# The end of the odd mixer: who splits the up weights, who takes the last roots, and the order of the last half blocks

## What is computed

```python
for layer in range(DEPTH):
    g = norm_gains[layer]
    h = rmsnorm(x, g[0])
    mix = even_mixer(...) if layer % 2 == 0 else odd_mixer(h, w_qkv, sinks, w_out, cos, sin)
    x = x + rmsnorm(mix, g[1])
    h = rmsnorm(x, g[2])
    x = x + rmsnorm(conv_ffn(h, ffn_w_in[layer], ...), g[3])

def rmsnorm(x, g):
    return x * lax.rsqrt(jnp.mean(x * x, axis=-1) + EPS) * g
```

## Time and profile before

| | us |
|---|---|
| timed runs, median of 3 | 2566.87 |
| timed runs, lowest and highest | 2565.96 and 2571.13 |
| the profiled execution | 2568.79 |
| its span in the trace | 2567.0 |

### The profile page before, as it was taken

How to read it: one execution, slowest core, us unless ns; L and a number is a source line. 1 busy time by engine, 2 the same in 40 slices (tenths; PEclk the granted TensorE clock), 3 DMA queues, 4 the chain that set the end, 5 groups by cost and what they waited for, 6 DMA issues and landing times. The chain is left out here.

```text
span 2567.0 us, 31771 instructions
## 1 busy us (share of the span) xinstructions
PE 2373.3 (92%) x11619; PEld 1983.1 (77%) x11619; DVE 1671.2 (65%) x2408; ACT 1189.6 (46%) x1881; POOL 912.7 (36%) x670
## 2 busy tenths in 40 slices
PE   6889878989899899999999979899879999999998
PEld 5668667889777688888787867688767888887886
DVE  4564667865544788888636744556577888884365
ACT  4444777766533343443425532455423443443354
POOL 2101103401011688888200001132258888870000
PEclk9999988999999899999999989979989999999999
DMA  4001101000041122222664731221112222237475
GB/s 147 26 25 42 33 1 42 26 1 2 30 168 59 57 91 82 80 85 82 211 211 167 247 107 41 52 64 50 67 54 81 79 90 83 76 102 252 154 254 180
DMA packets 183156, 237.47 MB, mean 93 GB/s; under 512 B 14132, under 2 KB 135316, under 8 KB 183004
## 3 DMA queue, kind: packets, MB, share of 16 engines
q1 hardware_dynamic: 177440, 217.94, 26.2%
q10 hardware_dynamic: 5564, 17.52, 1.7%
HBM read 195.48 MB, written 39.94 MB: 92 GB/s over the span
## 5 line engine op out<-in xcount | busy, mean ns | idle before, releaser
L126 PE MATMUL l_ps<-l_t_hi,l_s_hi 128*128 128x512 f32 x480 | 186.7, 389 | 0.0
L126 PE MATMUL l_ps<-l_t_lo,l_s_hi 128*128 128x512 f32 x480 | 186.7, 389 | 0.0
L126 PE MATMUL l_ps<-l_t_hi,l_s_lo 128*128 128x512 f32 x480 | 186.7, 389 | 0.0
L2230 POOL TENSOR_TENSOR l_s_lo<-l_raw,l_s_hi 128x512 fp32r<-128x512 f32 x100 | 157.2, 1580 | 45.8 <-ACT l_s_hi L2134 45.8
L2230 POOL TENSOR_TENSOR l_s_lo<-l_w_sum,l_s_hi 128x512 fp32r<-128x512 f32 x80 | 168.6, 2128 | 6.1 <-ACT l_s_hi L2134 3.7
L2506 DVE TENSOR_TENSOR l_wlo<-l_raw,l_whi 128x1024 fp32r<-128x1024 f32 x68 | 83.2, 1223 | 101.2 <-ACT l_whi L2068 101.2
L194 POOL TENSOR_TENSOR wring_w_lo<-wring_raw,wring_w_hi 128x1024 fp32r<-128x1024 f32 x22 | 52.5, 2390 | 258.9 <-ACT wring_w_hi L190 258.9
L2068 ACT ACTIVATE l_whi<-l_raw 128x1024 fp32r<-128x1024 f32 x76 | 80.3, 1056 | 126.6 <-PE l_ps L126 118.9
L126 PE MATMUL l_ps<-odd_act_hi,l_s_hi 128*128 128x512 f32 x320 | 125.6, 392 | 11.5 <-POOL l_s_lo L2230 11.5
L126 PE MATMUL l_ps<-rest_hi,l_s_hi 128*128 128x512 f32 x320 | 125.6, 393 | 11.5 <-POOL l_s_lo L2230 11.5
L126 PE MATMUL l_ps<-rest_lo,l_s_hi 128*128 128x512 f32 x320 | 125.4, 392 | 0.0
(11 more groups left out here) (415 smaller groups left out, 6963.7 us busy)
## 6 DMA issues: line engine op xcount, KB each, us to landing
l_raw<-in_ffn_w_out SPq DMA_DIRECT2D x68, 512.0 KB, 4.2
l_raw<-in_ffn_w_in SPq DMA_DIRECT2D x48, 512.0 KB, 4.7
gated_dram<-l_gate_out SPq DMA_DIRECT2D x44, 512.0 KB, 2.6
l_gated<-gated_dram SPq DMA_DIRECT2D x88, 256.0 KB, 4.1
l_rawl<-in_ffn_w_out SPq DMA_DIRECT2D x44, 512.0 KB, 4.4
wring_raw<-in_even_w_in SPq DMA_DIRECT2D x20, 512.0 KB, 3.8
l_raw_g<-in_ffn_w_in SPq DMA_DIRECT2D x20, 512.0 KB, 3.8
l_raw_v<-in_ffn_w_in SPq DMA_DIRECT2D x20, 512.0 KB, 4.8
```

The costliest lines, as they stand in the source:

```text
L126: mm = pe.matmul(o, w, m, start=a, stop=z)
L2230: pool.tensor_tensor(s_lo[m % NW][:], weight_of(r, q), s_hi[m % NW][:].bitcast(F32), ALU.subtract).then_inc(s_lo_done, 1)
```

## The change

- **Roots.** For blocks 6 and 7 (`LAST` = 6), both norms: ACT takes the square root behind its square (`root`), and DVE takes the reciprocal (`inverse`) ahead of its scaling. POOL's `rsqrt` stays for blocks 0 to 5.
- **Splits.** The low parts of up tiles 0, 1 and 2 are made by DVE (`up_lo_part`), POOL makes tile 3's only.
- **ACT's end in a new order.** Behind slot 35: `take_y(7)`, `first(7)`, `split_w(1)`, h12, h13, `second(7)`, `split_w(2)`, h14, h15. Before, `split_w(1)` and h12 stood between `take_y(7)` and `first(7)`.
- **DVE's end written out** in the order low part of tile 0, h12, `first(7)`, tile 1, h13, `second(7)`, tile 2, h14, h15.
- **PE.** Half of `up_half(0, 0)` stands ahead of the turn of h13, half behind it.
- **A bank of its own.** h15 is turned into O, the bank of the attention's outputs, and waits only for the attention to have left it.

```diff
@@ OddFront
+    LAST = TB - 2
+    def bank_of(self, kind, i):
+        return self.O if (kind, i) == ("h", 2 * TB - 1) else self.U
@@ scalar
+        def root(i, b, squared):
+            sc.wait_ge(squared, b + 1)
+            sc.activation(self.var[i][:, b:b + 1], self.ss[i][:, b:b + 1], ACT.Sqrt, bias=self.g.const[:, K_EPS:K_EPS + 1],
+                          scale=1.0 / D).then_inc(self.root_done[i], 1)
@@ scalar, in first and in second, behind the square
+            if b >= self.LAST:
+                root(0, b, self.sq1)
@@ scalar, the slot loop
-        for n in range(self.LAST_SLOT + 11):
+        for n in range(self.LAST_SLOT):
-            if n in (self.LAST_SLOT - 1, self.LAST_SLOT, self.LAST_SLOT + 3):
-                split_w(min(n - self.LAST_SLOT + 1, 2))
+            if n == self.LAST_SLOT - 1:
+                split_w(0)
+        take_y(TB - 1)
+        first(TB - 1)
+        split_w(1)
+        part_hi("h", 2 * TB - 4)
+        part_hi("h", 2 * TB - 3)
+        second(TB - 1)
+        split_w(2)
+        part_hi("h", 2 * TB - 2)
+        part_hi("h", 2 * TB - 1)
@@ gpsimd
-        for b in range(TB):
+        for b in range(self.LAST):
-                if b == TB - 1:
-                    up_lo(i)
@@ turn_parts
+            u = self.bank_of(kind, i)
+            if u is self.O:
+                pe.wait_ge(self.O_taken, self.NG)
@@ vector
+        def inverse(i, b, ready):
+            dve.wait_ge(self.root_done[i], b - self.LAST + 1)
+            dve.reciprocal(self.rstd[i][:, b:b + 1], self.var[i][:, b:b + 1]).then_inc(ready, 1)
@@ vector, behind the slot loop
+        up_lo(0)
+        part_lo("h", 2 * TB - 4)
+        first(TB - 1)
+        up_lo(1)
+        part_lo("h", 2 * TB - 3)
+        second(TB - 1)
+        up_lo(2)
+        part_lo("h", 2 * TB - 2)
+        part_lo("h", 2 * TB - 1)
@@ trunk_stage, tensor
                     odd.tensor(pe)
+                    pe.wait_ge(odd.h_lo_done, TB)
+                    pe.wait_ge(up_lo, 1)
+                    pe.wait_ge(odd.exp_done, odd.NG)
+                    up_half(0, 0, range(0, KT // 2))
                     odd.turn_parts(pe, odd.LAST_SLOT + 2)
-                    for u in range(2):
-                        pe.wait_ge(up_lo, u + 1)
-                        up_half(u, 0)
+                    up_half(0, 0, range(KT // 2, KT))
+                    pe.wait_ge(up_lo, 2)
+                    up_half(1, 0)
@@ trunk_stage, vector
+                def up_lo_part(u):
+                    dve.wait_ge(whi_done, u + 1)
+                    dve.tensor_tensor(wlo[u][:], raw_up[u % 2][:], whi[u][:].bitcast(F32), ALU.subtract).then_inc(up_lo, 1)
```

More of the change, by code:

```diff
@@ L772, in __init__ @@
         self.y_done, self.y_taken = st.sem("y_done"), st.sem("y_taken")
+        self.root_done = [st.sem(f"root_done{i}") for i in range(2)]
         self.h_turned, self.h_hi_done, self.h_lo_done = st.sem("h_turned"), st.sem("h_hi_done"), st.sem("h_lo_done")
@@ L916, in part_hi @@
         def part_hi(kind, i):
+            u = self.bank_of(kind, i).rearrange("p (k q) -> p k q", k=4)
             if kind == "o":
@@ L920, in part_hi @@
                     sc.wait_ge(self.y_done, 4 * i - 4)
-                sc.activation(self.o_part(self.o_hi, i), self.U.rearrange("p (k q) -> p k q", k=4), ACT.Copy).then_inc(self.o_hi_done, 1)
+                sc.activation(self.o_part(self.o_hi, i), u, ACT.Copy).then_inc(self.o_hi_done, 1)
             else:
                 sc.wait_ge(self.h_turned, i + 1)
-                sc.activation(self.h_part(self.new_act.hi, i), self.U.rearrange("p (k q) -> p k q", k=4), ACT.Copy).then_inc(self.h_hi_done, 1)
+                sc.activation(self.h_part(self.new_act.hi, i), u, ACT.Copy).then_inc(self.h_hi_done, 1)
+        def root(i, b, squared):
+            sc.wait_ge(squared, b + 1)
+            sc.activation(self.var[i][:, b:b + 1], self.ss[i][:, b:b + 1], ACT.Sqrt, bias=self.g.const[:, K_EPS:K_EPS + 1],
+                          scale=1.0 / D).then_inc(self.root_done[i], 1)
         def take_y(b):
@@ L942, in second @@
             sc.activation(self.junk[:], self.x[:], ACT.Square, accum_out=self.ss[1][:, b:b + 1]).then_inc(self.sq2, 1)
+            if b >= self.LAST:
+                root(1, b, self.sq2)
         hi(0)
@@ L1133, in turn_parts @@
             at = [x[:2] for x in self.uses].index((kind, i))
-            if at:
+            u = self.bank_of(kind, i)
+            if u is self.O:
+                pe.wait_ge(self.O_taken, self.NG)
+            elif at:
                 was, j = self.uses[at - 1][:2]
@@ L1148, in turn_parts, with vector @@
                 for k in range(4):
-                    mm = pe.transpose(self.U[:, k * P:(k + 1) * P], self.h[:, (4 * half + k) * P:(4 * half + k + 1) * P], ident)
+                    mm = pe.transpose(u[:, k * P:(k + 1) * P], self.h[:, (4 * half + k) * P:(4 * half + k + 1) * P], ident)
                 mm.then_inc(self.h_turned, 1)
-    def vector(self, dve):
+    def vector(self, dve, up_lo):
         N_KEY, N_V, N_Q, N_ALL, NG, g = self.N_KEY, self.N_V, self.N_Q, self.N_ALL, self.NG, self.g
@@ L1208, in part_lo @@
         def part_lo(kind, i):
-            u = self.U.rearrange("p (k q) -> p k q", k=4)
+            u = self.bank_of(kind, i).rearrange("p (k q) -> p k q", k=4)
             if kind == "o":
@@ L1219, in first @@
                 dve.wait_ge(self.gain_in, 32)
+            if b >= self.LAST:
+                inverse(0, b, self.iv1)
             dve.wait_ge(self.iv1, b + 1)
@@ L1227, in second @@
         def second(b):
+            if b >= self.LAST:
+                inverse(1, b, self.iv2)
             dve.wait_ge(self.iv2, b + 1)
@@ L2232, in _ @@
                 if odd:
-                    odd.gpsimd(pool, lo)
-                for u in range(2 if odd else 0, 3):
+                    odd.gpsimd(pool)
+                for u in range(0 if odd else 3):
                     lo(u)
@@ L2260, in turn, with up_half @@
                     mm.then_inc(turned, 1)
-                def up_half(u, h):
-                    for k in range(KT):
+                def up_half(u, h, rows=range(KT)):
+                    for k in rows:
                         mm = three_passes(pe, [ps[u % 4][:, H[h]]], whi[u % 3][:, k, :], wlo[u % 3][:, k, :],
```

8 lines of the change are left out of this document (3 added, 5 removed).

## The result

The changed kernel takes 2554.76 us (median of 4 runs, 2553.36 to 2555.28); the kernel before, on the same chip, 2569.00 (4 runs, 2565.96 to 2572.81). The ratio is 0.9939, interval 0.9924 to 0.9954: faster by 0.5 to 0.8%. Forecast were 2555.2 us, 11.7 less than the 2566.87 measured for the kernel before until then.

A forecast was written before the change was run, and what follows sets the result against it. The last half block's low part was taken to set the clock, through POOL's and DVE's token sums, for PE's unbroken 367 us. 11.5 us earlier there plus 0.17 at ACT's tap, sum 11.7: 2566.87 to 2555.2 us, range 2551.5 to 2560.5.

The forecast's parts named there:

- Block 6, first norm: First root on ACT at 1844.70 us behind a hidden table load, scaling at about 1846.95 instead of 1847.02: gain 0.1.
- rule on draining: At ACT's table load: about 1.38 us of draining beside the 1.28; the sum would stay between 10.9 and 11.7 us.
- Block 6, second norm: Scaling at 1852.7 us taking 1.28, `h_ready` 7 at 1854.0 where before it was 1858.1: gain 4.1.
- Block 7: First scaling at 1858.95 us against 1864.39, second from 1863.6 to 1864.9 against an end at 1877.57: gain so far 12.7.
- PE is late next: PE ends `up_half(1, 0)` at 1868.1 us, though `odd_h` is ready since 1864.9, before turning h14: 3.2 us lost.
- 16th low part: h15's low part, the last of the half blocks, over at 1870.75 us instead of about 1882.25: 11.5 us earlier.
- Behind it: From h15's low part to the first product the chain moves whole; ACT's tap gains 0.17 us more, sum 11.7.
- given back: Rival: a link ahead of or behind the first product doesn't move; 2558 to 2567 us, chance 0.07.
- The collisions aren't the cause: Rival: block 7's two scalings stay at 3.34 us for another reason; gain 9.6, time 2557.3, chance 0.03.
- PE at its lower level through the moved matmuls: Rival: all 48 matmuls of the first halves at granted 0.50; gain 1.5, time 2565.4, chance of most 0.05.
- slower: Rival: lower level from 1855 us on through the 96 matmuls of tiles 2 and 3; 2582 us, chance 0.03.

The follow-up runs named there:

- early turns: Changed kernel with h14 and h15 turned in the middle of `up_half(1, 0)` instead of behind it: 2556.08 us, ratio 0.9944 to the kernel before; run again 2556.99, 0.9952.

## Why the prediction was right

All moments below are moved by 1.81 us, so that the last `o` half starts at 1846.09 as before.

- **Block 6, first norm.** The root was forecast at 1844.70 and came at 1844.69; the scaling at 1846.88 (forecast 1846.95). The table load is hidden, as forecast. The rule on draining, weighed there, of the Trainium skill ("ScalarE: Activation LUTs", section "What ACT_TABLE_LOAD costs") isn't borne out: the root stands 0.02 us behind the load, and `h_ready` 7 isn't later.
- **Block 6, second norm.** Scaling at 1852.63 and 1.28 long, `h_ready` 7 at 1853.9 (forecast 1852.7 and 1854.0).
- **Block 7.** First scaling at 1858.95, second at 1863.61 (forecast 1858.95, and 1863.6).
- **PE is late next.** Forecast were 3.2 us between `h_ready` 8 and the turn; it was 3.4. The early turns show that this was a real gate, since cutting it brought 2.75 us.
- **16th low part.** Over at 1870.87 (forecast 1870.75), that is 1869.06 in the changed kernel's own time: 11.4 us earlier than the 1882.23 of before, where 11.5 was forecast. `up_half(1, 0)` began at 1862.69 and the turn at 1868.31, 5.62 us. The prediction priced it at 5.5 and then stepped 5.4 (1862.7 to 1868.1), a slip of 0.1; and its 0.22 for a matmul, busy time over count in the earlier trace rows, is a little low: in that stretch matmuls start 0.227 us apart, in `up_half(1, 0)` 0.234 on average. Of this miss of 0.2, the largest of the sum, 0.1 is left at the end, since the eight transposes took 1.03 instead of two times 0.64.
- **Behind it.** 0.17 us were forecast to be won at the tap, 0.27 came: from the low part's end to the first product it is 1914.93 - 1869.06 = 45.87, and it was 1928.37 - 1882.23 = 46.14. Nothing was given back, 638.57 us to the end against 638.63.

Forecast 11.7, measured 11.63 in S. That the **median** of 2554.76 lies only 0.4 us from the forecast is luck. Forecast was 2555.2 on a median of 2566.87 for before; with a fourth run that median is 2569.00, and the difference of the medians is 14.2 us (12.8 where the changed kernel ran again). The profiled span shows what such a difference can hold: 11.63 from the change, 0.06 behind it, and 1.81 from ahead of it.

The rivals. *The collisions aren't the cause* fell by three kernels: 1.28 without POOL's split, 2.77 with another read on POOL, 1.28 with its writes. *PE at its lower level through the moved matmuls* didn't come in the changed kernel, nor did *slower*, but their mechanism is real and close: with h13 turned first it cost 2.71 us, and with one scaling longer by 1.49 PE lost another 1.56. The prediction argued from gaps of 0.4 to 0.9 us and one of 1.4; they were 0.46, 0.77, 0.39 and 1.57. That argument was weaker than it looked: the kernel before ran at a granted clock of 0.52 from 1882 to 1886 us behind a gap of 1.41 (with one of 3.38 and one of 1.41 just ahead of it), and the last section has kernels with gaps below 3 us whose clock fell and others whose clock didn't. What it didn't say is that the order of PE is what kept them so small: half of `up_half(0, 0)` ahead of the turn brings 2.04 us by its place and 2.71 by the clock, more than h15's bank (1.48), and it has no line of its own in the prediction's sum. Without it roots, splits and bank together gave 6.88.

## What to carry to other kernels

Where an instruction of DVE that reads two tiles lasts longer than its equals, look for a POOL instruction that reads and began just ahead of it; moving the reader off POOL took 2.1 us from each, while a memset on POOL beside such an instruction cost nothing. When a chain becomes faster, ask which engine then gets to the meeting point last: the splits alone were worth 7.1 us and the roots alone 7.9, both with the bank 6.9 while PE kept its old order and 11.6 with the new one, and one more cut in PE's order brought 2.75 in S. And keep PE's waits short by putting work that is ready ahead of them, since a wait can be paid a second time in the clock behind it. Measure such edits between two marks in the trace, for the run times of one kernel here lie up to 11 us apart (2550.27 to 2561.43 with the early turns), mostly for reasons ahead of the code in question; and say so when, as with those early turns, the gain between the marks doesn't show in the time.

## What the runs showed of the hardware that was not expected

- The length of PE's waits doesn't say by itself whether the granted clock falls. It fell behind a wait of 4.42 us, behind one of 2.72 (with the roots alone, 0.59 in 1862 to 1866) and behind one of 1.88, but in no profile behind the 1.57 ahead of the last halves (1869.10 in the changed kernel, where the window behind it shows 1.00). Two waits of 1.41 us with the four transposes of h15 between them stand in three kernels behind an unbroken run of matmuls. With the roots alone and with h15 in U again the window behind them reads:

```profile
1878.70:1882.70 4.00, 4.00 (x12) 3.16 (x13) 1.32 (x1) 0.00 (x0) 3.98 (x4) 0.63 0.00 0
```

```profile
1870.00:1874.00 4.00, 3.94 (x17) 3.24 (x18) 1.24 (x2) 0.00 (x0) 3.92 (x4) 1.00 0.00 0
```

  With the splits alone it is 0.64 (1871.5 to 1875.5). What decides between these the runs don't show.
- The collision is symmetric. DVE behind POOL: 3.34 instead of 1.28, or 2.77, or 1.45; each time the scaling ends 1.07 to 1.09 us behind POOL's end, however much of it lay beside POOL. POOL behind DVE: 3.35 instead of 2.34. And it takes place between short instructions in a row too: beside POOL's sums DVE's 128 x 512 instructions take 1.7 to 1.8 us instead of 0.7.
- A DVE instruction that reads one tile in PSUM and one in SBUF isn't delayed by a split on POOL. In the changed kernel this one lies wholly inside POOL's `l_wlo` (1878.56 to 1880.97) and takes the same 1.28 us as ever:

```profile
1879.65 1.28 DVE L2480 SCALAR_TENSOR_TENSOR l_y_g<-l_ps,main_conv,l_y_g 128x1022 f32<-128x1022 f32 x1
```

- POOL's memset of a 128 x 1024 tile takes 0.95 us (the second began 0.89 us behind the first), and a scaling with two of them beside it took its 1.28.
